# Modulation columns by transposes of the accumulator and VectorE sums; gate rows by transposes of a column read with step zero

## The reference

```python
mod = silu(c) @ w_ada + b_ada
(sh1, s1, g1, shm, smx, gm, sh2, s2, g2) = split(mod, 9)
h = h + 0.5 * g1 * swiglu(rms(h) * (1 + s1) + sh1, ffn1)
h = h + gm * (concat[conv group, attention](rms(h) * (1 + smx) + shm) @ w_out)
h = h + 0.5 * g2 * swiglu(rms(h) * (1 + s2) + sh2, ffn2)
return rms(h) * g_final
```

## Time and profile before

| | us |
|---|---|
| median of 3 runs | 1921.9 (1918.92 to 1922.35) |
| the profiled execution | 1919.46 |
| its span in the profile | 1917.3 |
| PE busy in the span | 1840.7 (96%) |
| DVE busy | 1389.1 (72%) |
| POOL busy, ACT busy | 802.1, 796.2 (42% each) |

### The profile page before, as it was taken

One profiled execution on the slowest core, in us unless ns is written; L12 is line 12 of the kernel. 1 busy time (PEld: TensorE's weight loads), 2 busy tenths in 40 slices (PEclk: granted clock), 3 DMA queues, 4 the chain that ended last, 5 costly groups with the idle time before them and its releaser, 6 DMA issues.

```text
span 1917.3 us, 22679 instructions
## 1 busy us (share of the span) xinstructions
PE 1840.7 (96%) x8043; PEld 1471.1 (77%) x8043; DVE 1389.1 (72%) x1774; ACT 796.2 (42%) x1248; POOL 802.1 (42%) x605
## 2 busy tenths in 40 slices
PE   4999999999999999997999998999999999999997
PEld 3788888888888878985665656877888888888886
DVE  6778888885777686776888886358656555577778
ACT  4532232223344554246776643154332323334443
POOL 1076655665200010029999941014566556520000
PEclk8999999999999999997999999999999999999999
DMA  9046666545753442000000023112233323476333
GB/s 351 19 138 199 209 220 198 192 160 206 255 194 97 131 160 71 1 1 0 1 1 0 3 73 144 66 55 91 102 110 110 110 83 110 170 251 226 99 106 126
DMA packets 132795, 232.11 MB, mean 121 GB/s; under 512 B 8780, under 2 KB 66227, under 8 KB 132434
## 3 DMA queue, kind: packets, MB, share of 16 engines
q1 hardware_dynamic: 132500, 230.73, 35.5%
q10 hardware_dynamic: 190, 0.01, 0.0%
HBM read 177.75 MB, written 52.95 MB: 120 GB/s over the span
## 4 chain that ended last, share of the span: by engine, by line
PE 35%; POOL 7%; issue 6%; DVE 5%; DMA 1%; ACT 1%; POOLq 0%; ACTq 0%; DVEq 0%
PE ps L502 19%; PE ps L854 9%; PE ps L2753 4%; POOL cv L1816 3%; PE ps L376 1%; POOL cv L1815 1%; PE ps L1657 1%; POOL slot L1766 1%; PE ps L1635 1%; DVE T L935 1%; POOL rqk L1751 0%; DMA wor<-in_w_out 0%; DVE wo L1926 0%; DVE grow L1673 0%; DVE ring L479 0%
## 5 line engine op out<-in xcount | busy, mean ns | idle before, releaser
L502 PE MATMUL ps<-T,ring 128*128 128x512 f32 x1920 | 441.8, 389 | 0.0
L502 PEld LDWEIGHTS ps<-T,ring 128*128 128x128 f32 x1920 | 360.3, 188 | 75.1 <-DVE ring L479 0.2
L502 PE MATMUL ps<-B,ring 128*128 128x512 f32 x1440 | 339.6, 392 | 4.1 <-DVE SG L561 3.8
L502 PEld LDWEIGHTS ps<-B,ring 128*128 128x128 f32 x1440 | 270.5, 189 | 63.9 <-issue 8.0
L954 POOL TENSOR_SCALAR stat<-stat 128x1 f32<-128x1 f32 x32 | 10.5, 329 | 548.7 <-ACT XS L879 257.8
L568 POOL TENSOR_TENSOR HID<-HID,SG 128x512 f32<-128x512 f32 x80 | 122.1, 1527 | 262.3 <-DVE HID L553 151.5
L854 PE MATMUL ps<-PW 128*128 128x512 f32 x924 | 217.3, 389 | 0.0
L854 PE MATMUL ps<-PT 128*128 128x512 f32 x900 | 212.0, 390 | 0.0
L854 PEld LDWEIGHTS ps<-PW 128*128 128x128 f32 x924 | 173.3, 188 | 36.0
L479 DVE TENSOR_TENSOR ring<-sums,ring 128x512 fp32r<-128x512 f32 x160 | 162.4, 1024 | 52.6 <-ACT ring L473 52.6
L854 PEld LDWEIGHTS ps<-PT 128*128 128x128 f32 x900 | 168.5, 188 | 34.8
(11 more groups left out here) (337 smaller groups left out, 3313.1 us busy)
## 6 DMA issues: line engine op xcount, KB each, us to landing
adat<-ffn_hidden SPq DMA_DIRECT2D x154, 256.0 KB, 2.7
ada_raw<-in_w_ada SPq DMA_DIRECT2D x56, 512.0 KB, 4.0
rawg<-in_ffn_wg SPq DMA_DIRECT2D x22, 1024.0 KB, 5.5
rawu<-in_ffn_wu SPq DMA_DIRECT2D x22, 1024.0 KB, 5.3
ffn_hidden<-HID SPq DMA_DIRECT2D x84, 256.0 KB, 2.8
ffn_hidden<-base SPq DMA_DIRECT2D x66, 256.0 KB, 2.6
H<-in_x SPq DMA_DIRECT2D x16, 512.0 KB, 6.6
h_saved_rows<-H SPq DMA_DIRECT2D x16, 512.0 KB, 2.6
```

Source lines behind the costliest of these rows:

```text
L502: mm = e.matmul(ps[:, product_bank(M, k)], ring[:, place % RING, wx, kc], RIGHT[k][:, xx, kc], start=(kc == 0 and i == 0), stop=(kc == HC ...
```

## The change

For vectors 3 to 8, PE transposes the eight blocks of `ada_acc` in two halves of four (behind products 1 and 3 of e) into the one free PSUM bank, and DVE sums each half along its free axis into `modc` (at k = 2 and k = 4, before the product's own reads), and adds the bias at k = 4. The eight pieces of the next vector are each added one product later. For the gate rows PE transposes the column itself, read with step zero as a 128x128 block, eight times; the diagonal on DVE goes.

```diff
-        def pe_ada_sum(e, v):
-            e.wait_ge(ada_step, v * KC + KC)
...
-            for j in range(KC):
-                mm = e.matmul(ps[:, MISC, j:j + 1], ada_acc[:, j * P:(j + 1) * P], ones[:, 0:1], start=True, stop=True)
-            mm.then_inc(acc_used, 2)
+        def pe_ada_turn(e, v, h):
+            if h == 0:
+                e.wait_ge(ada_step, v * KC + KC)
...
+            else:
+                e.wait_ge(ada_half, 2 * (v - SHM) + 1)
+            for j in range(HC):
+                at = (h * HC + j) * P
+                mm = e.transpose(ps[:, MISC, j * P:(j + 1) * P], ada_acc[:, at:at + P], ident[:])
+            mm.then_inc(acc_used, 1)
+
+        def dve_ada_sum(e, v, h):
+            e.wait_ge(acc_used, 2 * v - 1 + h)
+            e.tensor_reduce(modc[:, v * KC + h * HC:v * KC + (h + 1) * HC], ps[:, MISC].rearrange("p (j n) -> p j n", j=HC),
+                            AX_X, ALU.add).then_inc(ada_half, 1)
...
-            e.tensor_tensor(modc[:, cols], ps[:, MISC, 0:KC], vect[:, cols], ALU.add).then_inc(mod_ok, 1)
+            e.tensor_tensor(modc[:, cols], modc[:, cols], vect[:, cols], ALU.add).then_inc(mod_ok, 1)
...
-        def pe_row(e, r, row=grow):
-            e.wait_ge(row_src, r + 1)
+        def pe_row(e, v):
+            e.wait_ge(mod_ok, N_MOD - 1)
             for h in range(2):
-                mm = e.matmul(ps[:, ROW_BANKS[h]], ones[:], row[:, h * HALF:(h + 1) * HALF], start=True, stop=True)
+                for j in range(HC):
+                    col = v * KC + h * HC + j
+                    mm = e.transpose(ps[:, ROW_BANKS[h], j * P:(j + 1) * P], modc[:, col:col + 1].broadcast_to([P, P]), ident[:])
...
-                pieces = {(0, 3): (0,), (0, 4): (1,), (0, 5): (2,), (0, 6): (3,), (1, 0): (4,), (1, 1): (5,), (1, 2): (6,),
-                          (1, 3): (7,)} if ada_of(f, g) is not None else {}
+                pieces = {(0, 4): (0,), (0, 5): (1,), (0, 6): (2,), (1, 0): (3,), (1, 1): (4,), (1, 2): (5,), (1, 3): (6,),
+                          (1, 4): (7,)} if ada_of(f, g) is not None else {}
```

More of the change, by code:

```diff
@@ L204, in build @@
         ada_step = sem("ada_step")
-        row_src = sem("row_src")
+        ada_half = sem("ada_half")
         row_mm = sem("row_mm")
@@ L1089, in pe_gate1_half @@
             e.matmul(ps[:, MISC], ones[:], ada_acc[:, h * HALF:(h + 1) * HALF], start=True, stop=True).then_inc(acc_used, 1)
-        def pe_ada_sum(e, v):
-            e.wait_ge(ada_step, v * KC + KC)
-            if v == SHM:
-                e.wait_ge(col_half, 2)
-            else:
-                e.wait_ge(mod_ok, v - 1)
-            for j in range(KC):
-                mm = e.matmul(ps[:, MISC, j:j + 1], ada_acc[:, j * P:(j + 1) * P], ones[:, 0:1], start=True, stop=True)
-            mm.then_inc(acc_used, 2)
+        def pe_ada_turn(e, v, h):
+            if h == 0:
+                e.wait_ge(ada_step, v * KC + KC)
+                if v == SHM:
+                    e.wait_ge(col_half, 2)
+                else:
+                    e.wait_ge(mod_ok, v - 1)
+            else:
+                e.wait_ge(ada_half, 2 * (v - SHM) + 1)
[7 more added lines that the diff above has]
+                            AX_X, ALU.add).then_inc(ada_half, 1)
         def dve_ada_column(e, v):
-            e.wait_ge(acc_used, 2 * v)
+            e.wait_ge(ada_half, 2 * (v - SHM) + 2)
             cols = slice(v * KC, (v + 1) * KC)
-            e.tensor_tensor(modc[:, cols], ps[:, MISC, 0:KC], vect[:, cols], ALU.add).then_inc(mod_ok, 1)
+            e.tensor_tensor(modc[:, cols], modc[:, cols], vect[:, cols], ALU.add).then_inc(mod_ok, 1)
         def dve_gate1_row(e, h):
@@ L1495, in dve_ffn @@
                 g, m = divmod(M, 2)
-                pieces = {(0, 3): (0,), (0, 4): (1,), (0, 5): (2,), (0, 6): (3,), (1, 0): (4,), (1, 1): (5,), (1, 2): (6,),
-                          (1, 3): (7,)} if ada_of(f, g) is not None else {}
+                pieces = {(0, 4): (0,), (0, 5): (1,), (0, 6): (2,), (1, 0): (3,), (1, 1): (4,), (1, 2): (5,), (1, 3): (6,),
+                          (1, 4): (7,)} if ada_of(f, g) is not None else {}
                 for k in range(PRODUCTS_OF):
-                    made = made_in(f, g) if m == 0 and k in (1, 2, 3) else None
+                    made = made_in(f, g) if m == 0 and 1 <= k <= 4 else None
                     if made == G1 and k < 3:
@@ L1506, in dve_ffn @@
                             dve_half_row(e, f)
-                    elif made not in (None, G1) and k == 3:
-                        dve_ada_column(e, made)
+                    elif made not in (None, G1) and k in (2, 4):
+                        dve_ada_sum(e, made, k // 2 - 1)
                     if f is fs[1] and M == ROW_M:
-                        if k == 0:
-                            dve_row_diag(e, G2)
-                        elif k == 2:
+                        if k == 2:
                             dve_row_copy(e, 1)
@@ L1523, in dve_ffn @@
                         dve_cut(e, f, k - 4)
+                    if made not in (None, G1) and k == 4:
+                        dve_ada_column(e, made)
                     for kc in pieces.get((m, k), ()):
@@ L1559, in pe_ffn @@
                         pe_gate1_half(e, k)
-                    elif (m, k) == (0, 1) and made is not None:
-                        pe_ada_sum(e, made)
+                    elif m == 0 and k in (1, 3) and made not in (None, G1):
+                        pe_ada_turn(e, made, k // 2)
                     if f is fs[1] and M == ROW_M and k == 1:
                         e.wait_ge(*f.w_out(out_made(ROW_M - 1, "V")))
-                        pe_row(e, 1)
+                        pe_row(e, G2)
         NU = 2 * NH
@@ L2677, in _ @@
             e.wait_ge(z_lo, 6)
-            pe_row(e, 0, gm_row)
+            pe_row(e, GM)
             e.wait_ge(up_lo, 2)
```

4 lines of the change are left out of this document (removed).

## The result

| | before | after |
|---|---|---|
| median, us | 1921.1 (1918.6 to 1925.0, 6 runs) | 1932.1 (1931.4 to 1932.9, 6 runs) |
| the profiled execution, its span | 1919.46, 1917.3 | 1932.28, 1930.5 |
| PE busy in the span | 1840.7 (96%) | 1839.4 (95%) |
| DVE busy | 1389.1 (72%) | 1392.4 (72%) |

The ratio is 1.0068, with a 95% interval of 1.0056 to 1.0081: the change costs 11 us, where +4.8 was forecast. The time lies just above the range. PE has as much work as before, DVE 3 us more in the whole span, and PE stands idle for 91.1 us of the span in place of 76.6: the loss is in waits.

A forecast was written before the change was run, and what follows sets the result against it. DVE's loop from C12 of o to C12 of o was taken to bound FFN 1. Columns +6.0 and gate rows -1.2 gave +4.8 us, added to the 1921.9 median: 1926.7, range 1916 to 1932.

The forecast's parts named there:

- groups 3 to 8: FFN 1, six DVE loops: +0.9 us per group, 41.9 for DVE's loop against 39.0 for PE, in all +5.4.
- gate rows: g2 and gm rows made by transposes, DVE's diagonals worth nothing: together -1.2 us, bounds 0 and -1.7.
- PE's cost of the transposes: PE in FFN 1: four transposes cost 0.45 us, two halves 0.9 in place of 1.85 for the fp32 products.
- Rival D: Transposes cost PE its clock: 12 passes at half speed after each of 12 sets, 1.6 us each, 1936; chance 0.03.
- The e half: DVE in e of FFN 1: second sum +0.6, one piece leaves, bias at nothing; 19.75 us against 20.53, -0.8.
- The o half: DVE in o of FFN 1: a sixth piece, partly taken up by DMA waits; 22.2 us against 20.5, +1.7.
- The other chain, by pieces 5 and 7: In o, landings of 3.95 us for pieces 5 and 7 put C12 at 22.05 us behind C12 of e.
- rival C: Long landings, 4.7 us and more: o is 23.6, the loop +2.3, in all +13.2, 1935; chance 0.09.
- Group 2, +0.2: FFN 1's group 2 has no column to make; one piece leaves e and comes into o: about +0.2 us.
- Rival A: The pause for DMAs takes up the sixth piece: o stays at 20.5, in all -5.4, 1916.5; chance 0.18.
- The g2 row, -0.8: PE at g2's gate row: eight transposes cost 0.9 us in place of 1.73 for four passes, PE never idle there.
- The gm row, -0.4: At gm's gate row PE's 0.8 us is hidden behind DVE's GLU read; the copies start at most 0.4 earlier.

The follow-up runs named there:

- e5: The changed kernel with the old table of pieces, the second sum at k = 3 and the bias at product 3 of o: 1917.2 us, ratio 0.9988.
- e1: The kernel before with only the new table of pieces (each added one product later), fp32 products and gate rows as before: 1929.9 us, ratio 1.0048.
- e4: The changed kernel with the bias addition moved to product 3 of o, piece 0 waiting for the transposes alone: 1933.0 us, ratio 1.0065.
- e2: The changed kernel with the DMA of piece 6 issued ahead of the 1 MB load of rawu: 1935.4 us, ratio 1.0076.
- e10: The changed kernel with each piece's DMA cut from 512 KB to 64 KB, DVE's instructions keeping their size: 1917.1 us, ratio 0.9985.

## Why the prediction was wrong in size, step by step

The profiled executions differ by 13.2 us of span, where +4.8 was worked out. By stages: FFN 1's group 2 +1.6 (forecast +0.2), groups 3 to 8 +13.1 (+5.4), group 9 +0.3 (+0.45), gate rows -0.9 (-1.2). That is +14.1. The start of the kernel is 1.8 longer and the mixer 2.4 shorter in this execution; the change does not touch the first of these places, and in the mixer only the gm row. Of the 2.4, about 0.9 lies near 905 us, where the trace of before has 7.0 us near half clock and the new one 3.5; the rest I can't explain. With these two places the sum is 13.5.

- **PE's cost of the transposes** (0.45 a set): right (0.38). Rival D is not the cause. From 170 us on, FFN 1 has four stretches near half clock (178, 304, 348 and 434 us) where before it had the one at 417.70; this is the one at 348, with the granted clock of 0.61 behind the engines' busy times:

```profile
348.17:352.50 4.33, 4.33 (x12) 3.43 (x13) 4.33 (x5) 0.00 (x0) 4.19 (x3) 0.61 0.62 188
```

Each stands behind a wait of PE, the first of 1.8 us and the others of 2.6. DVE's loop covers those at 304 and 348: the e halves that begin with them take 19.82 and 19.80 us, those of groups 4 and 5, without one, 19.82 and 19.85, and PE waits for the next C12 all the same. e5, with as many transposes, shows none, and e1, without a transpose in the columns, shows four (258, 302, 343 and 428 us; 0.52 was granted from 302 to 305.5).
- **The e half, -0.8**: right in its sum (-0.74), by luck in two of its terms. The sums take 0.68 each, near the 0.6 they were given, and the first is in the pause. But the second lengthens the half by hardly anything: e1, without sums, has e at 19.37, and e4, with both sums and the bias out of the way, at 19.45. The bias addition, costed at nothing, is worth 0.4 (e4), and the two errors cancel. It waits for GpSimd as the Trainium skill has it ("SBUF — State Buffer", section "SBUF: two separate sides"): two SBUF inputs, 1.25 us in place of 0.15, even for 8 columns. The trace agrees with the rule; in group 7 the addition ends when GpSimd's instruction of line L582, begun before it, has ended:

```profile
359.20 1.83 POOL L582 TENSOR_TENSOR HID<-HID 128x512 f32<-128x512 f32 x1
...
359.81 1.25 DVE L1113 TENSOR_TENSOR modc<-modc,vect 128x8 f32<-128x8 f32 x1
```

- **The o half, +1.7: this is the step that failed.** It came to +2.9. The mechanism was right: two buffers, so that each piece waits for the one two before it and a landing, and C12 by the chain of piece 6. The term of it that was mis-sized is the landing of piece 6, "I give it 5.0". The working had C12 at 17.2 plus that landing, and the 17.2 holds in every group (17.22 to 17.26). The landing measured 5.8 to 7.1, 6.15 in the mean of groups 3 to 8. Six times 1.15 is 6.9 of the 7.7 us by which these groups went beyond the forecast. Before, with the load 3.3 us ahead, piece 6 landed in 3.9 to 5.2 (the 5.4 of the old rows was a piece 4, 19 us behind the load); with the load only 1.4 us ahead I took less than the longest of those. The other chain, by pieces 5 and 7, lies just behind and does not bind: with piece 6 this late, piece 7 no longer waits. The 23.6 of rival C, to which I gave 0.09, came nearer in number only, since it had pieces 5 and 7 land in 4.7, and they took 3.6 to 4.9.
- **Group 2, +0.2**: the same error. A piece leaves e and comes into o there as well, and that half takes 24.3 against 21.0, with piece 6 landing in 7.03.
- **Rival A** (the pause takes the sixth piece up) is out by the result itself, 2.45 us of waits in place of 0.92 in the o half of group 7, and by e1, where the new table alone brings o to 23.3.
- **The g2 row, -0.8**: right. Before, the row's four passes and the 12 behind them took 4.45; in the changed kernel 3.63:

```profile
1465.42 1.03 PE L1129 MATMUL ps<-ident,modc 128*128 128x128 f32 x8
1466.21 3.00 PE L502 MATMUL ps<-B,ring 128*128 128x512 f32 x12
1469.05 9.23 PE L502 MATMUL ps<-T,ring 128*128 128x512 f32 x40
```

- **The gm row, -0.4**: it gave nothing. The copies start right behind DVE's GLU read, without their old wait of 0.40, but PE goes on when that read is out, as before: 0.8 us behind its start (858.02, 858.85), as with 841.21 and 842.0. What comes behind the copies was not on the path.

What stays open: why piece 6 lands in 5.8 us in one group and in 7.1 in another, at the same place in the list (o follows it), and most of the -2.4 us in the mixer.

## What to carry to other kernels

In a loop with two buffers, count the time from "buffer free" to "data used" for each piece, and price a DMA that goes out just behind a large one on the same queue above the median landing: here the median stayed at 3.9, and the one in each group that bound the loop took 5.8 to 7.1, more than the longest landing before the change (5.4). A term on which six loops hang is worth a measurement of its own. Work taken from the engine that is busiest in the profile is worth nothing where another engine's loop sets the pace; look first for what that loop's engine stands still for, and fill it: the first addition moved into a pause, and three others forward, gained 5 us, where the cheaper transposes, with the pieces moved later for them, lost 11. Moving such a queue entry ahead of its neighbour handed the delay to the next one (e2). And two costs that end at the same moment, as in e10, each look like the whole cause; look at what the engine would have waited for next.

## What of the hardware I had not expected

- A DVE addition of 128x8 with two SBUF inputs takes 1.25 us each time (six of six) where GpSimd works beside it, and 0.15 where it doesn't or where one input is PSUM. The reductions of 128x512 from PSUM beside it take 0.68 each time.
- A DMA of 64 KB took 4.0 to 5.6 us to land, 1.4 us behind one of 1 MB on the same queue (seven of seven); the others of its kind took 1.7 to 2.6.
- A piece that arrives earlier can run longer: 2.32 in place of 1.28 us, since it then meets a GpSimd instruction.
